# Mixing loop of a hybrid attention and RWKV-7 block: the order of TensorE's work inside one iteration's solve, and the place of the sixth projection

## The chip, the cores and the metric

The kernel runs on one core of one Trainium2 chip. The metric is device time in microseconds (us); runs of one kernel are compared by their median. The engines are TensorE (PE in the profile, with its weight loads as PEld), VectorE (DVE), ScalarE (ACT), GpSimd (POOL) and SyncE (SP), which issues the DMAs. Each engine works through its own instructions in their written order and waits on semaphores.

## The reference, cut to what matters

One layer over a sequence of 1024 tokens of width 1024, all float32:

```python
x += 0.5 * swiglu(rmsnorm(x), w_gate1, w_up1, w_down1)
z = rmsnorm(x) @ w_in                     # q, ak, av, r, k, v, u, ug, gate_a, gate_b
o_a = window_gqa_sinks(q, ak, av, sinks)  # 16 heads, window of two 64-token chunks, ALiBi
o_b = rwkv7_time_mix(r, k, v, ...)        # per head a 64x64 state:
      # sa = state @ a_t
      # state = state * w_t + sa b_t^T + v_t k_t^T ;  y_t = state @ r_t
x += (sigmoid(gate_a) * o_a + sigmoid(gate_b) * o_b) @ w_out
x += cross_attention(rmsnorm(x), rmsnorm(mem))
x += 0.5 * swiglu(rmsnorm(x), w_gate2, w_up2, w_down2)
out = rmsnorm(x)
```

The change touches only the second step, where attention and time mixing are computed together. The time mixing is done in chunks of 64 tokens. Inside a chunk the recurrence is a triangular system, which is solved by doubling the solved blocks (levels 2, 4, 8, 16, 32); from chunk to chunk a 64x64 state is carried in a chain.

## The kernel before, in words

`mixer()` runs 16 iterations (`ITER`), one for each pair of heads (8) and half of the sequence (2 halves of 512 tokens, 8 chunks each), and two more that drain the pipeline. Iteration i does three things at a time: it projects the inputs of pair i+1, it solves the triangular systems of pair i, and it carries the chain and writes the outputs of pairs i-1 and i-2. Every engine has `prepare(i)` and then `solve(i)`.

**Projections.** An iteration has six units (`PROJ`: k, r, v, q, ga, gb). A unit is 24 matmuls of 128x512 on two-part rounded operands (L1171), accumulated in bank P0 or P1 by turns. For each unit SP loads a weight panel, ACT rounds it (`round_panel`, L1442), POOL subtracts to get the low part (`subtract_panel`, L1076), PE multiplies, and ACT stores the result (`store`, L1451, L1455, L1459). In the kernel before, units 0 to 4 are in PE's `prepare`. Unit 5 is done in `solve`, in five pieces of 4 or 5 matmuls, one in each level; ACT stores it, and rounds the panel after next, after its `solve`, and POOL subtracts that panel after its `solve`. Pair 8 (the first of the second half) needs the second half of the normed input, which SP loads into the same buffer as the first one (`load_second_half`, L1048) once the last unit of the first half is projected (`proj_ready` of 48); unit 48 waits for it (`s_half`).

**Solve, head.** Eight slots: (0) the products N and its transpose (64 small matmul instructions each way, banks F0 and F3), (1, 2) b scores in two halves (L1279), (3) b tokens, (4, 5) k scores in two halves (L1279), (6) v tokens, (7) k tokens. ACT copies N (L1533, L1535) and the tokens (L1539, L1542, L1545); DVE masks N (L1756), the b scores (L1721) and the start of the solution (L1724), and the k scores (L1729); POOL masks and completes the start X0 (L1128, L1131) and masks N for each level (L1137).

**Solve, levels.** Five levels of four quarters: Z of chunks 0 to 3, Z of chunks 4 to 7 (PE; ACT copies each, L1557), growth of chunks 0 to 3, growth of chunks 4 to 7 (PE; DVE adds into XT, L1743, and into X, L1749). Z and the growth into XT write from one half of the array to the other (`to_other`, L1291), the growth into X does not (`heads`, L1158), and the two alternate.

**Chain.** The pair before is carried over its 8 chunks in 3 steps each, 24 in all. Step 0 multiplies the old state (ACT copies the product p1, L1550), step 1 solves for sa (ACT copies, L1553), step 2 sums the new state (DVE updates it, L1768). Each step needs the copy or the update of the step before. Step s-4 follows slot s: four steps stand in the head after slots 4 to 7, and in a level the first two stand between the matmuls of the two Z quarters, the third after the first growth and ahead of the piece of the projection, the fourth after the second growth.

**Attention.** The scores of pair i are the first thing in PE's `prepare(i)` (banks F2, F3); DVE scales them (L1614). After them come the two small LoRA products (L1197, L1198).

In `prepare(i)` POOL takes the token differences (L1098) for DVE's mixes (L1601), and two transposes on PE (L1241) wait for a spread that DVE copies (L1677).

Of the kernel before, what the change touches and what calls it, by code (L numbers as in the profile page):

```python
# [35 lines left out]
ALU = mybir.AluOpType  # L36
# [54 lines left out]
def build(nc, d, out, x_spill, m_spill, h_spill, a_spill):  # L91
    table, where = constants()
    ctx = ExitStack()
    with ctx:
# [832 lines left out]
        def mixer():  # L927
# [71 lines left out]
            SCORES, FIRST_CHAIN = 8, 4  # L999
            SLOTS = SCORES + 4 * len(LEVELS)  # L1000
            assert SLOTS == FIRST_CHAIN + 3 * NC
            TERMS = 3 * KT

            def quarter(s):

                return divmod(s - SCORES, 4)
# [13 lines left out]
            with nc.Block() as block:  # L1020
# [49 lines left out]
                def _(pool):  # L1070
# [12 lines left out]
                    def prepare(i):  # L1083
# [39 lines left out]
                        for j in range(3, NP - 1):  # L1123
                            next_panel(i, j)
# [20 lines left out]
                    for i in range(ITER + 2):  # L1145
                        prepare(i)
                        if i < ITER:
                            solve(i)
                        next_panel(i, NP - 1)

                @block.tensor
                def _(pe):
# [7 lines left out]

                    def project(unit, first=0, end=TERMS):

                        if first == 0:
                            pe.wait_ge(S("panel_low"), unit + 1)
                            if unit >= 2:
                                pe.wait_ge(S("proj_stored"), unit - 1)
                        for term in range(first, end):
                            kt, (wp, hp) = term // 3, THREE[term % 3]
                            if unit == NP * PAIRS and term % 3 == 0:
                                pe.wait_ge(s_half[kt], 32)  # L1170
                            last = mm(bank[:, unit % 2, :], pw[wp][:, unit % 2, kt], hA[hp][:, kt],  # L1171
                                      start=term == 0, stop=term == TERMS - 1)
                        if end == TERMS:
                            last.then_inc(S("proj_ready"), 1)

                    def prepare(i):
# [23 lines left out]
                        if more:  # L1200
                            project(first)
# [14 lines left out]
                        if more:  # L1216
                            project(first + 1)
# [37 lines left out]
                        if more:  # L1255
                            project(first + 4)

                    def solve(i):
# [35 lines left out]
                        def score_slot(s):  # L1294
                            every = range(NC)
                            if s == 0:
                                seen("rows_ready", 4, 4)
                                seen("oa_ready")
                                for n in every:
                                    heads(one(F0)[:, n, :], cur[:, n, 0, :], b_ch[:, n, :])  # L1300
                                    last = to_other(one(F3)[:, n, :], cur[:, n, 0, :], b_ch[:, n, :])
                                last.then_inc(S("n_ready"), 1)
                            elif s == 1:
                                scores(F1, b_ch, 0).then_inc(S("b_scores_ready"), 1)
                            elif s == 2:
                                seen("bonus_used")
                                scores(F2, b_ch, 1).then_inc(S("b_scores_ready"), 1)
                            elif s == 3:
                                seen("ends_ready", 2, 2)
                                if i + 1 < ITER:  # L1310
                                    pe.wait_ge(S("proj_stored"), NP * (i + 1) + 4)
                                by_heads(P1, lambda n: b_ch[:, n, :], lambda n: cur[:, n, 2, :],
                                         every).then_inc(S("b_tok_ready"), 1)
                            elif s == 4:
                                seen("x_copied")
                                scores(F3, k_ch, 0).then_inc(S("k_scores_ready"), 1)
                            elif s == 5:
                                if i + 1 < ITER:
                                    pe.wait_ge(S("proj_stored"), NP * (i + 1) + 5)
                                scores(P0, k_ch, 1).then_inc(S("k_scores_ready"), 1)  # L1320
                            elif s == 6:
                                seen("n_stored")
                                seen("n_copied")
                                by_heads(F0, lambda n: vm[:, n * CH:(n + 1) * CH], lambda n: c("stack_ident"),
                                         every).then_inc(S("v_tok_ready"), 1)
                            else:
                                seen("base_stored", 2, 1)
                                by_heads(F1, lambda n: k_ch[:, n, :], lambda n: cur[:, n, 2, :],
                                         every).then_inc(S("k_tok_ready"), 1)

                        def level_slot(n, k, beside=None):
                            q = k % 2
                            chunks = range(4 * q, 4 * q + 4)
                            if k < 2:
                                if n == 0:
                                    seen("xt0_ready", 2, q + 1)
                                    if q == 0:
                                        seen("base_stored", 2, 2)
                                    else:
                                        seen("before_stored", 2, 1)  # L1340
                                else:
                                    seen("n_masked", 4, n)
                                    seen("xt_added", 10, 2 * n - 1 + q)
                                for m, at in enumerate(chunks):
                                    last = to_other(one(ZB[q])[:, m, :], n_st[n % 2][:, at, :], xt_new[:, at, :])
                                    if m == 3:
                                        last.then_inc(S("z_ready"), 1)
                                    if beside and m > 0:
                                        chain_step(*beside, m - 1)
                            else:  # L1350
                                seen("z_stored", 10, 2 * n + 1 + q)
                                if n == 0:
                                    seen("x0_ready")
                                    seen("v_tok_stored")
                                    seen("k_tok_stored")
                                else:
                                    seen("x_added", 8, 2 * n)
                                if q == 1:
                                    seen("xt_added", 10, 2 * n + 1)
                                    if n < 4:  # L1360
                                        seen("x_added", 8, 2 * n + 1)
                                for m, at in enumerate(chunks):
                                    grown = to_other(one(TB)[:, m, :], x_st[:, at, :], z_st[:, at, :])
                                    if m == 3:
                                        grown.then_inc(S("xt_grown"), 1)
                                    if n < 4:
                                        last = heads(one(XB)[:, m, :], z_st[:, at, :], x_st[:, at, :])
                                if n < 4:
                                    last.then_inc(S("x_grown"), 1)
# [36 lines left out]
                        for s in range(SLOTS):  # L1406
# [845 lines left out]
```

## Time and profile before

| | |
|---|---|
| median of 3 runs | 3304.08 us (3301.25 to 3305.58) |
| the profiled execution's own time | 3303.52 us |
| its span in the profile | 3301.7 us |
| PE busy | 2963.9 us, 90% |
| PEld busy | 2434.4 us, 74% |
| DVE busy | 1598.2 us, 48% |
| POOL busy | 1300.2 us, 39% |
| ACT busy | 1055.4 us, 32% |

The first view of the profile gives each engine's busy time over the span. An engine's own waits are in the view of waits, and the order of its instructions, with their starts, in the timeline. The mixing loop takes the stretch from about 863 to 2050 us. Its iterations can be told apart by the two LoRA products (L1197), which begin at 1461.6, 1531.9, 1602.1 us and so on.

### The profile page before, as it was taken

Reading aid. Unit: us, or ns where it says so; the run is one execution under the profiler, and the core shown is the slowest. Engines: PE = TensorE matmul, PEld = TensorE weight load, DVE = VectorE, ACT = ScalarE, POOL = GpSimd, SP = SyncE. Lnnn points to the kernel's source line nnn. Section 1 sums busy time; section 2 is a strip of 40 time slices with the busy share of each in tenths; the row PEclk is TensorE's granted clock in tenths of the full one; section 3 lists DMA queues with packets and bytes.
Section 4 is the critical chain, followed back from the end, with each engine's and each line's share of the span. In section 5 each row is a group of like instructions: output and inputs, shape, how many; then the busy total and the mean of one; then the engine's idle time right before and its main releaser. Section 6 shows DMA issues by size and latency. Waiting matters only on the chain. (4 is left out here: it accounts for less than half of the span.)

```text
span 3301.7 us, 61575 instructions
## 1 busy us (share of the span) xinstructions
PE 2963.9 (90%) x26974; PEld 2434.4 (74%) x26974; DVE 1598.2 (48%) x1747; ACT 1055.4 (32%) x1718; POOL 1300.2 (39%) x667
## 2 busy tenths in 40 slices
PE   3899999996899999999999986797976799999995
PEld 2688888884678877787877765786755588887885
DVE  6654444444166556656655662113222744453445
ACT  2433333222234334433434432212121333333221
POOL 1344444442364545455544541222131344444441
PEclk7999999997999999999999986898988899999997
DMA  3222224433221111322111100611002222234441
GB/s 139 80 96 80 80 103 166 144 121 134 59 62 58 52 45 45 96 63 63 52 45 45 53 21 9 229 52 32 19 26 89 64 80 77 78 108 159 144 144 67
DMA packets 247432, 270.71 MB, mean 82 GB/s; under 512 B 13184, under 2 KB 204800, under 8 KB 245120
## 3 DMA queue, kind: packets, MB, share of 16 engines
q1 hardware_dynamic: 247168, 266.81, 24.6%
q8 instruction: 212, 3.47, 0.4%
q14 instruction: 52, 0.43, 0.0%
HBM read 218.54 MB, written 48.23 MB: 81 GB/s over the span
## 5 line engine op out<-in xcount | busy, mean ns | idle before, releaser
L459 POOL TENSOR_TENSOR w_low<-ffn_work,w_high 128x1024 fp32r<-128x1024 f32 x182 | 445.0, 2446 | 668.6 <-ACT w_high L532 393.9
L499 PE MATMUL bank<-h_high,w_high 128*128 128x512 f32 x1232 | 484.6, 393 | 57.6 <-DVE h_low L643 34.6
L499 PE MATMUL bank<-h_low,w_high 128*128 128x512 f32 x1232 | 483.3, 392 | 0.0
L499 PE MATMUL bank<-h_high,w_low 128*128 128x512 f32 x1232 | 482.9, 392 | 0.0
L1076 POOL TENSOR_TENSOR mix_panel_low<-arena,mix_panel_high 128x1024 fp32r<-128x1024 f32 x96 | 233.0, 2427 | 343.6 <-ACT mix_panel_high L1442 343.6
L1171 PE MATMUL bank<-mix_h_high,mix_panel_high 128*128 128x512 f32 x768 | 317.6, 414 | 20.0 <-POOL mix_panel_low L1076 14.9
L690 DVE TENSOR_TENSOR h_low<-ffn_work,h_high 128x512 fp32r<-128x512 f32 x88 | 205.7, 2337 | 250.7 <-ACT h_high L547 250.7
L499 PEld LDWEIGHTS bank<-h_high,w_high 128*128 128x128 f32 x1232 | 233.9, 190 | 110.9 <-issue 60.1
L1171 PE MATMUL bank<-mix_h_low,mix_panel_high 128*128 128x512 f32 x768 | 304.4, 396 | 0.0
L1171 PE MATMUL bank<-mix_h_high,mix_panel_low 128*128 128x512 f32 x768 | 303.3, 395 | 0.0
L516 PE MATMUL bank<-h_high,w_high 128*128 128x512 f32 x704 | 275.2, 391 | 4.6 <-DVE h_low L690 4.6
L516 PE MATMUL bank<-h_low,w_high 128*128 128x512 f32 x704 | 275.3, 391 | 0.0
L516 PE MATMUL bank<-h_high,w_low 128*128 128x512 f32 x704 | 275.1, 391 | 0.0
L499 PEld LDWEIGHTS bank<-h_high,w_low 128*128 128x128 f32 x1232 | 233.6, 190 | 49.0
L499 PEld LDWEIGHTS bank<-h_low,w_high 128*128 128x128 f32 x1232 | 233.7, 190 | 48.3
L674 DVE TENSOR_TENSOR ffn_work<-bank,ffn_work 128x512 f32<-128x512 f32 x132 | 90.2, 688 | 346.2 <-ACT ffn_work L574 244.5
L459 POOL TENSOR_TENSOR w_low<-arena,w_high 128x1024 fp32r<-128x1024 f32 x60 | 145.1, 2420 | 195.8 <-ACT w_high L532 195.8
L1291 PE MATMUL bank<-arena 64*64 64x64 f32 x5120 | 214.5, 226 | 2.4 <-DVE arena L1749 0.9
L1291 PEld LDWEIGHTS bank<-arena 64*64 64x64 f32 x5120 | 179.2, 134 | 30.8 <-issue 29.0
L1171 PEld LDWEIGHTS bank<-mix_h_high,mix_panel_high 128*128 128x128 f32 x768 | 145.0, 189 | 68.7 <-issue 27.4
L540 ACT ACTIVATE w_high<-ffn_work 128x1024 fp32r<-128x1024 f32 x88 | 93.2, 1059 | 310.4 <-PE bank L516 303.7
L685 DVE TENSOR_TENSOR ffn_work<-ffn_work 128x512 f32<-128x512 f32 x66 | 153.7, 2328 | 69.4 <-ACT ffn_work L584 68.8
(263 smaller groups left out, 5822.8 us busy)
## 6 DMA issues: line engine op xcount, KB each, us to landing
arena<-w_in SPq DMA_DIRECT2D x96, 512.0 KB, 3.8
ffn_work<-w_down SPq DMA_DIRECT2D x88, 512.0 KB, 3.6
a_spill<-ffn_work SPq DMA_DIRECT2D x88, 256.0 KB, 2.3
ffn_work<-a_spill SPq DMA_DIRECT2D x88, 256.0 KB, 2.7
ffn_work<-w_gate SPq DMA_DIRECT2D x12, 1024.0 KB, 5.7
ffn_work<-w_up SPq DMA_DIRECT2D x12, 1024.0 KB, 8.2
arena<-x_spill SPq DMA_DIRECT2D x3, 4096.0 KB, 14.2
arena<-w_gate SPq DMA_DIRECT2D x10, 1024.0 KB, 5.6
```

The lines of the kernel that those rows point to most:

```text
L459: nc.gpsimd.tensor_tensor(slot(w[1], q), src, slot(w[0], q).bitcast(F32), ALU.subtract).then_inc(s_low, 1)
L499: last = mm(bank[:, bk, :], w[wp][:, q % RING, kt, e], h[hp][:, k, kt], start=fresh and kt + wp + hp == 0, stop=kt == KT // 2 - 1 and wp = ...
L516: last = mm(bank[:, BANK_OF[o], :], w[wp][:, (LAST + p) % RING].rearrange("p a b c -> p (a b) c")[:, o], h[ap][:, B11, p % 4], start=p % N ...
L540: A(slot(w[0], LAST + p), panel[p % 4].rearrange("p (a b) -> p a b", b=P), ACT.Copy).then_inc(s_high, 1)
L674: V.tensor_tensor(post[first + e], bank[:, bk[e], :], post[first + e], ALU.add).then_inc(s_added, 1)
L685: ins = V.tensor_tensor(post[at], post[at], post[at + 1], ALU.mult)
L690: V.tensor_tensor(h[1][:, B11, p % 4], a_raw[p % 2], h[0][:, B11, p % 4].bitcast(F32), ALU.subtract).then_inc(s_alow, 1)
L1076: G.tensor_tensor(pw[1][:, unit % 2], raw[unit % 2], pw[0][:, unit % 2].bitcast(F32), ALU.subtract).then_inc(S("panel_low"), 1)
L1171: last = mm(bank[:, unit % 2, :], pw[wp][:, unit % 2, kt], hA[hp][:, kt], start=term == 0, stop=term == TERMS - 1)
L1291: last = mm(hs(out, 1 - e), hs(lhs, e), hs(rhs, e), start=True, stop=True)
```

## The change

The sixth projection (unit 5) moves from the levels of the solve to the end of `prepare`, behind the fifth, as one block; ACT's store and rounding and POOL's subtraction for it move with it. The two halves of the k scores, the v tokens, the k tokens and the attention scores of the next iteration move into the levels, one to each, where the pieces of the projection were (`filler`). The chain's four steps of the head stand one ahead of each of the four remaining parts of the head, and the fourth step of a level stands ahead of the second growth. Banks of some scores change. The core of the diff:

```diff
                     def prepare(i):
...
                         if live:
-                            pe.wait_ge(S("proj_stored"), NP * i + 4)
-                            for n in range(NC):
-                                at = (window + n) * CH
-                                last = heads(two(F2)[:, n, :], q_t[:, n * CH:(n + 1) * CH], kd[:, g, at:at + P])
-                            last.then_inc(S("att_scores_ready"), 1)
+                            if i == 0:
+                                attention_scores(0)
...
                         if more:
                             project(first + 4)
+                            project(first + 5)
...
+                        def filler(n):
+                            if n == 0:
+                                seen("base_stored", 2, 2)
+                                scores(P0, k_ch, 0).then_inc(S("k_scores_ready"), 1)
+                            elif n == 1:
+                                seen("b_tok_stored")
+                                scores(P1, k_ch, 1).then_inc(S("k_scores_ready"), 1)
+                            elif n == 2:
+                                seen("before_stored", 2, 1)
+                                by_heads(P0, lambda n: vm[:, n * CH:(n + 1) * CH], lambda n: c("stack_ident"),
+                                         every).then_inc(S("v_tok_ready"), 1)
+                            elif n == 3:
+                                seen("before_stored", 2, 2)
+                                by_heads(P1, lambda n: k_ch[:, n, :], lambda n: cur[:, n, 2, :],
+                                         every).then_inc(S("k_tok_ready"), 1)
+                            elif i + 1 < ITER:
+                                seen("z_stored", 10, 10)
+                                attention_scores(i + 1)
...
-                            if live and i + 1 < ITER and s >= SCORES and quarter(s)[1] == 2:
-                                n = quarter(s)[0]
-                                if n == 0:
-                                    seen("b_tok_stored")
-                                project(NP * (i + 2) - 1, n * TERMS // 5, (n + 1) * TERMS // 5)
...
+                        if live:
+                            hop(0)
+                            n_products()
+                            hop(1)
+                            b_scores(0)
+                            hop(2)
+                            b_scores(1)
+                            hop(3)
+                            b_tokens()
+                            for n in range(len(LEVELS)):
+                                make_z(n, 0)
+                                make_z(n, 1)
+                                grow(n, 0)
+                                hop(FIRST_HOPS + 4 * n + 2)
+                                filler(n)
+                                hop(FIRST_HOPS + 4 * n + 3)
+                                grow(n, 1)
```

`make_z` keeps two chain steps between the matmuls of the two Z quarters (`hop` 4 and 5 of level 0, and so on). On ACT, POOL and DVE:

```diff
@@ ACT
                         next_unit(4)
+                        next_unit(5)
...
                         if live:
+                            hop(0)
                             seen("n_ready")
                             A(flat(x_st), bank[:, F3, :], ACT.Copy).then_inc(S("x_copied"), 1)
+                            hop(1)
...
-                        if i + 1 < ITER:
-                            store(NP * (i + 2) - 1)
-                            round_panel(NP * (i + 2) + 1)
@@ POOL
-                        for j in range(3, NP - 1):
+                        for j in range(3, NP):
                             next_panel(i, j)
...
-                        next_panel(i, NP - 1)
@@ DVE
+                            store_base(0)
+                            hop(2)
+                            store_base(1)
+                            for n in range(len(LEVELS)):
+                                hop(FIRST_HOPS + 4 * n)
+                                hop(FIRST_HOPS + 4 * n + 1)
+                                level_slot(n, 0)
+                                hop(FIRST_HOPS + 4 * n + 2)
+                                hop(FIRST_HOPS + 4 * n + 3)
+                                if n < 2:
+                                    store_before(n)
+                                level_slot(n, 1)
```

ACT copies the v tokens after the chain steps of level 2 and the k tokens after those of level 3.

## Rows read from the trace of the kernel before

**Rows 1.** Page, busy time of each engine over the span: us, share, instructions.

```profile
PE 2963.9 (90%) x26974; PEld 2434.4 (74%) x26974; DVE 1598.2 (48%) x1747; ACT 1055.4 (32%) x1718; POOL 1300.2 (39%) x667
```

**Rows 2.** Windows, two iterations: length, busy us (instructions), PEclk the granted clock.

```profile
1461.60:1531.90 70.30, 68.50 (x1182) 56.30 (x1180) 43.70 (x65) 28.34 (x59) 35.63 (x23) 1.00 0.18 53
1383.60:1461.60 78.00, 71.52 (x1182) 56.94 (x1180) 41.49 (x66) 28.35 (x59) 34.47 (x23) 0.98 0.35 106
```

**Rows 3.** Waits of PE, 1461.6 to 1954 us (seven iterations): total, times, longest.

```profile
PE bank L1158 <- DVE mix_work L1768: 3.3, 7, 0.5
PE bank L1241 <- DVE mix_work L1677: 3.2, 7, 0.5
```

**Rows 4.** Timeline of PE around one projection piece: start, us, instruction, [idle before].

```profile
1513.56 0.28 PE L1158 MATMUL bank<-mix_work,arena 64*64 64x64 f32 x4
1513.78 0.50 PE L1171 MATMUL bank<-mix_h_low,mix_panel_high 128*128 128x512 f32 x1
1514.12 0.39 PE L1171 MATMUL bank<-mix_h_high,mix_panel_low 128*128 128x512 f32 x1
1514.35 0.40 PE L1171 MATMUL bank<-mix_h_high,mix_panel_high 128*128 128x512 f32 x1
...
1515.14 0.27 PE L1291 MATMUL bank<-arena 64*64 64x64 f32 x2
```

**Rows 5.** Timeline of PE, head of the solve and the first growth.

```profile
1498.32 0.27 PE L1158 MATMUL bank<-mix_work 64*64 64x64 f32 x2
...
1499.30 1.92 PE L1279 MATMUL bank<-mix_work 64*64 64x128 f32 x32
1501.05 1.10 PE L1158 MATMUL bank<-mix_work 64*64 64x64 f32 x32
1501.98 1.04 PE L1279 MATMUL bank<-mix_work 64*64 64x128 f32 x16
...
1507.16 0.27 PE L1158 MATMUL bank<-mix_work,arena 64*64 64x64 f32 x2 [0.17 <-ACT mix_work L1550]
...
1508.12 0.27 PE L1158 MATMUL bank<-arena 64*64 64x64 f32 x2
```

**Rows 6.** Timeline of PE where one level ends and the next begins.

```profile
1511.13 0.28 PE L1291 MATMUL bank<-arena 64*64 64x64 f32 x4
1511.63 0.27 PE L1158 MATMUL bank<-mix_work 64*64 64x64 f32 x2 [0.22 <-ACT mix_work L1553]
...
1515.85 0.28 PE L1291 MATMUL bank<-arena 64*64 64x64 f32 x3
1516.60 0.28 PE L1158 MATMUL bank<-mix_work,arena 64*64 64x64 f32 x2 [0.47 <-DVE mix_work L1768]
```

**Rows 7.** Timeline of DVE and POOL where the next iteration's mix begins.

```profile
1530.81 2.35 POOL L1076 TENSOR_TENSOR mix_panel_low<-arena,mix_panel_high 128x1024 fp32r<-128x1024 f32 x1 [11.60 <-ACT mix_panel_high L1442]
1534.45 1.51 DVE L1601 SCALAR_TENSOR_TENSOR mix_work<-mix_work,arena 128x512 f32<-128x512 f32 x1 [1.25 <-POOL mix_work L1098]
```

**Rows 8.** Timeline of ACT after the fifth projection, and one sa copy.

```profile
1498.43 0.60 ACT L1459 ACTIVATE mix_work<-bank 128x512 f32<-128x512 f32 x1
...
1499.87 0.59 ACT L1533 ACTIVATE arena<-bank 128x512 f32<-128x512 f32 x1
...
1507.54 0.22 ACT L1553 ACTIVATE mix_work<-bank 128x64 f32<-128x64 f32 x1 [0.43 <-PE bank L1158]
```

**Rows 9.** Timeline of DVE in the head of the solve.

```profile
1501.12 1.57 DVE L1724 TENSOR_TENSOR arena<-arena 128x256 f32<-128x256 f32 x1
1502.61 0.68 DVE L1721 TENSOR_TENSOR arena<-bank,arena 128x512 f32<-128x512 f32 x1
...
1505.46 0.28 DVE L1768 SCALAR_TENSOR_TENSOR mix_work<-mix_work,bank 128x64 f32<-128x64 f32 x1 [0.34 <-PE bank L1158]
```

**Rows 10.** Timeline of POOL in the head of the solve.

```profile
1500.05 2.36 POOL L1076 TENSOR_TENSOR mix_panel_low<-arena,mix_panel_high 128x1024 fp32r<-128x1024 f32 x1 [6.35 <-ACT mix_panel_high L1442]
...
1503.72 1.34 POOL L1131 TENSOR_TENSOR arena<-arena 128x512 f32<-128x512 f32 x1
```

**Rows 11.** Timeline of SP and PE where the second half comes in.

```profile
1380.88 0.34 SPq L1048 DMA_DIRECT2D mix_h_high<-h_spill  x1
...
1388.57 0.50 PE L1171 MATMUL bank<-mix_h_high,mix_panel_high 128*128 128x512 f32 x1 [2.99 <-DMA mix_h_low<-h_spill]
```

**Rows 12.** Timeline of PE in the last iteration, whose levels hold no projection.

```profile
1995.94 0.28 PE L1158 MATMUL bank<-mix_work,arena 64*64 64x64 f32 x4
1996.71 0.27 PE L1291 MATMUL bank<-arena 64*64 64x64 f32 x2 [0.48 <-DVE arena L1749]
```

More of the change, by code:

```diff
@@ L1159, in heads, with project, attention_scores @@
                         return last
[L1161 to L1169, printed above, removed]
-                                pe.wait_ge(s_half[kt], 32)
[L1171 to L1174, printed above, removed]
+                    def project(unit):
+                        if unit >= UNITS:
+                            return
+                        pe.wait_ge(S("panel_low"), unit + 1)
+                        if unit >= 2:
+                            pe.wait_ge(S("proj_stored"), unit - 1)
+                        for kt in range(KT):
+                            if unit == NP * PAIRS:
+                                pe.wait_ge(s_half[kt], 32)
+                            for wp, hp in THREE:
+                                last = mm(bank[:, unit % 2, :], pw[wp][:, unit % 2, kt], hA[hp][:, kt],
+                                          start=kt + wp + hp == 0, stop=kt == KT - 1 and wp == 1)
+                        last.then_inc(S("proj_ready"), 1)
+                    def attention_scores(i):
+                        pe.wait_ge(S("proj_stored"), NP * i + 4)
+                        for n in range(NC):
+                            at = (i // PAIRS * NC + n) * CH
+                            last = heads(two(F2)[:, n, :], q_t[:, n * CH:(n + 1) * CH],
+                                         kd[:, i % PAIRS // 4, at:at + P])
+                        last.then_inc(S("att_scores_ready"), 1)
                     def prepare(i):
@@ new lines, in solve, with n_products, b_scores @@
+                        every = range(NC)
+                        def n_products():
+                            seen("rows_ready", 4, 4)
+                            seen("oa_ready")
+                            for n in every:
+                                heads(one(F0)[:, n, :], cur[:, n, 0, :], b_ch[:, n, :])
+                                last = to_other(one(F3)[:, n, :], cur[:, n, 0, :], b_ch[:, n, :])
+                            last.then_inc(S("n_ready"), 1)
+                        def b_scores(q):
+                            if q == 1 and i + 1 < ITER:
+                                pe.wait_ge(S("proj_stored"), NP * (i + 2) - 1)
+                            scores((F1, P0)[q], b_ch, q).then_inc(S("b_scores_ready"), 1)
@@ new lines, in make_z @@
+                        def make_z(n, q):
+                            chunks = range(4 * q, 4 * q + 4)
+                            if n == 0:
+                                seen("xt0_ready", 2, q + 1)
+                                seen("n_stored")
+                                if q == 0:
+                                    seen("bonus_used")
+                                else:
+                                    seen("x_copied")
+                            else:
+                                seen("n_masked", 4, n)
+                                seen("xt_added", 10, 2 * n - 1 + q)
+                            for m, at in enumerate(chunks):
+                                last = to_other(one(ZB[q])[:, m, :], n_st[n % 2][:, at, :], xt_new[:, at, :])
+                                if m == 3:
+                                    last.then_inc(S("z_ready"), 1)
+                                if back and 0 <= m - q < 3:
+                                    chain_step(*divmod(FIRST_HOPS + 4 * n + q, 3), m - q)
@@ new lines, in grow @@
+                            if q == 1:
+                                seen("xt_added", 10, 2 * n + 1)
+                                if n < 4:
+                                    seen("x_added", 8, 2 * n + 1)
+                            for m, at in enumerate(chunks):
+                                grown = to_other(one(TB)[:, m, :], x_st[:, at, :], z_st[:, at, :])
+                                if m == 3:
+                                    grown.then_inc(S("xt_grown"), 1)
+                                if n < 4:
+                                    last = heads(one(XB)[:, m, :], z_st[:, at, :], x_st[:, at, :])
@@ L1371, in outputs @@
+                            if n < 4:
+                                last.then_inc(S("x_grown"), 1)
                         def outputs(n, part=None):
```

193 lines of the change are left out of this document (67 added, 126 removed).

## The prediction

> **What bounds the kernel now.** I read the page first: PE is busy 90% of the span, every other engine under half [rows 1]. Then the windows of single iterations of the mixing loop: one takes 70.3 us, PE is busy in 68.5 of them at full granted clock, and the next engine, DVE, in 43.7 [rows 2]. So PE's own order of work sets the loop's time, and a change that only moves work on the others is worth nothing unless PE waits for them. Third, PE's waits: few and short, some 0.5 us each in every iteration for the chain's state update and for the spread of the variance [rows 3]. The reader should not stop there: a small matmul counts as busy for 0.22 to 0.28 us while the next one can start 0.03 us later, so this view shows a wait only from where the last matmul has drained. The true loss is in PE's timeline, between the starts of neighbours. I therefore price everything from starts.
>
> **Part 1, the sixth projection becomes one block.** Inside a block one matmul starts 0.23 us after the other (1514.12 to 1514.35). A piece of five is entered and left at a price: from the last group of small matmuls (1513.56, four in about 0.12) to the next small one at 1515.14 there are 1.46 us, and five matmuls at 0.23 are 1.14 [rows 4]. That is 0.32 to 0.33 a piece, five pieces an iteration: 1.65 us saved, since at the end of prepare the block follows another projection and adds no border. The 24 matmuls themselves cost the same. The panel for it is rounded after unit 3 and subtracted while unit 4 runs, so PE should not wait for it. The parts put into the levels are the same instructions as before; their work cancels.
>
> **Part 2, chain steps apart.** Where a level ends with a chain step and the next one begins with its successor, PE stands: 1511.13 to 1511.63 for four matmuls worth 0.12, so 0.38 lost to ACT's copy of sa; and 1515.85 to 1516.60, 0.66 lost to DVE's state update [rows 6]. The steps' kinds repeat every three levels, so the first stands twice and the second once in an iteration. With the second growth between the two steps (16 pairs of the N products' kind took 0.98 [rows 5], so its 8 take 0.5) all three go: 2 x 0.38 + 0.66 = 1.42 us. The waits between the two steps of the Z quarters stay as they are, since those steps stay where they were but for one matmul.
>
> **Part 3, the prepare.** POOL's subtraction at 1530.81 stands ahead of the differences, and DVE's first mix waits 1.25 for them and is then slow at 1.51 [rows 7]; after the change POOL has nothing before them and takes them during the solve, so DVE's chain runs about 2 us earlier against PE. The wait for the spread goes (3.2 over seven [rows 3]): 0.45 us. What is late next is DVE's scaling of the attention scores, which now waits only for DVE's last add; it starts 0.3 us later against the LoRA products, well inside the 2 us.
>
> **Part 4, the head, where I expect the losses.** Let T be the start of the first small matmul after the last projection (1498.32). Work: N products 0.98, b scores 0.87 a half, b tokens 0.93, so 0.12 for one pair of heads [rows 5]. ACT is now in front of the first chain copy with the store and the rounding of a panel: it stored at T+0.11 and was free at T+1.55 [rows 8]. PE does hop 0 (two pairs, 0.23) and the N products and stands at T+1.21 at hop 1, which needs p1: copy 0.22, resumed at T+1.83. Loss 0.62. Then hop 1 and b scores to T+2.82, hop 2 to 3.05, b scores to 3.93. Hop 3 needs the state from DVE, and DVE has the first L1721 and L1724 before it. L1721 takes 0.68 and starts at about T+3.0; L1724 took 1.57 and ended 0.28 after POOL's subtraction [rows 9, 10]; POOL ends that at T+4.09 again, so L1724 ends at about T+4.4, the update takes 0.28, PE resumes at T+4.72. Loss 0.8. Then five pairs of hop 3 (0.58) and b tokens, T+6.23. The copy of the b tokens (0.6, like L1459) now stands on ACT just ahead of the copies of hop 4 and Z: a loss of about 0.35 in the second Z. The first growth comes at T+7.7, and X0, which POOL completes at T+6.74 [rows 10], is in time. Before, the first growth was at 1508.12, T+9.8 [rows 5], with 3.6 us of scores and tokens that are now elsewhere and 0.47 of waits, one of them at 1507.16. So waits of 1.77 stand for 0.47: a cost of 1.3 us. Its ends: only X0 binds and the two chain waits vanish, 0.5; or both ACT's queue and DVE's double, 3.0.
>
> **Queues behind the new waits.** On DVE the k scores' mask (0.7) stands ahead of the second adds of levels 0 and 1 and may hold the next Z by 0.25 once; the attention scores must see the last Z copied, 0.1; and with fillers of 0.9 in place of 1.46 some round trips begin to show, 0.2: together 0.55, from 0 to 3.3. The upper end is the last iteration, whose levels have no filler: the second growth waits there from 1995.94 to 1996.71 for DVE's adds, 0.66 more than the four matmuls need [rows 12]; five of these are 3.3. A filler of 0.9 covers 0.66, which is why I stay near the low end.
>
> Sum of an ordinary iteration: -1.65 -1.42 -0.45 +1.3 +0.55 = -1.7 us. Fourteen of them (1 to 14): -24.
>
> A page of the Trainium skill ("SBUF — State Buffer", section "Who interferes with whom") says that a DVE instruction with two SBUF inputs is shut out for the whole of a GpSimd instruction that reads SBUF and began first. The end of L1724 0.28 after POOL's end agrees. By that rule the second L1724, behind L1131, would end only at about T+7.0 and hold the second Z by some 0.2 us, 3 us in all; the forecast leaves this out.
>
> **Part 5, once.** The second half is loaded after the last unit of the first half. That unit ended in the last level of iteration 6: the load's first issue is at 1380.88 and PE still stands for it at 1388.57 [rows 11], and the iteration takes 78.0 instead of 70.3 us [rows 2]. Now the unit ends ahead of the solve, and the solve lay from 1498.32 to the LoRA products at 1531.9 in its like; even cut by 5 us that is far more than the 7.7 us from the first issue to that wait's end, and nothing in that solve reads the buffer. The 7.7 us go but for 0.1: -7.6.
>
> **Part 6, the ends.** The last iteration has no projection, before or after; its levels get fillers where they had none: three waits like the one of rows 12 (2.0) and 1.42 as above, and no panel stands before its head: -3.5. The first has no chain, so it saves the 1.65 and loses about 2 waiting for X0: +0.5.
>
> Total -24 -7.6 -3.5 +0.5 = -34.6, say -35. The profiled execution took 3303.5 us, 0.6 under the median of the three runs, so both give the same: **3268 us**. For this case alone 3258 to 3278.
>
> **The rivals.**
> (a) *The waits move instead of going.* Step 2 saves nothing, because what ends last between levels is DVE's add into XT and not the chain. For it: in rows 12 the adds of a growth reach PE 0.77 after its last group of matmuls, and the second Z now comes about that soon behind the growth. Against: DVE's last add is done before the state update in rows 6. Per iteration -1.65 -0.45 +1.3 +0.55 = -0.25; with parts 5 and 6, -15: 3289 us.
> (b) *The head costs little.* DVE gets L1724 through before POOL and ACT's panel is early: cost 0.5 instead of 1.3, and no 0.55: -3.0 an iteration, -42 -10.6: 3251 us.
> (c) *The levels fall to the round trips (slower).* The fillers of 0.9 don't cover the trip over ACT and DVE between the two growths, and every level waits 0.66 as in rows 12, the chain's saving being taken by the same waits: -1.65 -0.45 +1.3 +3.3 = +2.5 an iteration, +35, less 8 for part 5: 3330 us. It decides from 0.3 us of new waits a level. Against it: the wait without any filler is only 0.66.
> (d) *Nothing much*: the losses of the head are 3.0 and those of the levels 0.7: +0.2 an iteration, less the once-only parts, 3296 us.
>
> **How the numbers follow.** Forecast 0.54, (a) 0.16, (b) 0.20, (c) 0.05, (d) 0.05. The range from 3243 to 3295 leaves out (c), half of (d) and the far side of (b). About 0.2% (6.6 us) is what a measurement can tell from no change. The forecast, (a), (b) and part of (d) are faster by more: 0.91. Within: 0.04. Slower, mostly (c): 0.05.
>
> **What would show it.** An iteration of about 68.6 us between LoRA products; iteration 7 the same as the others, no wait for the spilled half; PE's timeline without the jumps of 0.5 and 0.75 at level borders, but with new ones at hop 1 (ended by ACT's p1 copy) and hop 3 (ended by the state update) in the head; L1171 in blocks only; no wait at L1241. Wrong, if PE waits for a panel ahead of the sixth unit, if the granted clock in the loop falls from 1.00, or if the wait before a second growth appears in each level.

## The result, and the profile after

The changed kernel takes 3325.55 us (median of 5 runs, 3319.22 to 3328.55) against 3303.97 before; the ratio is 1.0064 with a 95% interval of 1.0049 to 1.0078. It is slower by 21.6 us where 35 us less were forecast, and outside the range.

The profiled execution took 3325.55 us, its span is 3323.8 us. The page's row of busy times answers to [rows 1]: PE does the same 26974 matmuls and is busy for less.

```profile
PE 2944.8 (89%) x26974; PEld 2442.2 (73%) x26974; DVE 1571.2 (47%) x1747; ACT 1051.2 (32%) x1718; POOL 1296.7 (39%) x667
```

The windows of one ordinary iteration after, whole and in its three parts (prepare, solve up to the first growth, from there to the LoRA products), answer to [rows 2]. Columns: length, busy us of PE, PEld, DVE, ACT and POOL, granted clock, DMA share, GB/s.

```profile
1544.80:1616.50 71.70, 67.39 (x1178) 56.97 (x1178) 41.66 (x66) 27.79 (x60) 35.30 (x22) 1.00 0.18 51
1586.30:1593.70 7.40, 6.19 (x213) 5.68 (x213) 3.17 (x6) 4.02 (x10) 5.64 (x4) 1.00 0.25 71
1593.70:1616.50 22.80, 19.70 (x761) 18.53 (x752) 7.57 (x28) 6.94 (x24) 7.51 (x8) 1.00 0.01 4
1544.80:1586.30 41.50, 41.50 (x220) 32.77 (x220) 30.91 (x32) 16.83 (x26) 22.15 (x11) 1.00 0.25 74
```

The same three parts of an iteration of the kernel before:

```profile
1461.60:1498.30 36.70, 36.26 (x196) 28.15 (x194) 31.69 (x31) 15.08 (x23) 24.52 (x15) 1.00 0.28 83
1498.30:1508.10 9.80, 9.63 (x309) 9.38 (x308) 5.63 (x8) 5.51 (x13) 6.17 (x4) 1.00 0.20 57
1508.10:1531.90 23.80, 22.61 (x690) 18.78 (x682) 6.37 (x26) 7.75 (x24) 4.94 (x4) 1.00 0.02 4
```

| part of an iteration, us | before | forecast | after |
|---|---|---|---|
| prepare (with the block after) | 36.7 | 41.8 | 41.5 |
| head, to the first growth | 9.8 | 7.7 | 7.4 |
| levels, to the LoRA products | 23.8 | 19.4 | 22.8 |
| sum | 70.3 | 68.9 | 71.7 |

The forecast column is the prediction's own terms, split by place: the levels lose the five pieces (24 x 0.23 and 1.65) and the border waits (1.42), and get 3.6 of scores and tokens and 0.55. Its sum is 0.3 over the prediction's 68.6: the T+7.7 of the head doesn't quite follow from the prediction's own terms, 9.8 - 3.6 + 1.3 = 7.5, and the rest is rounding. Two parts came out within 0.3 us. All of the error is in the levels. What stands there is in the view of PE's waits over seven iterations, which answers to [rows 3]: total, times, longest. Most is given to "issue", time in which the profile shows nothing that PE waited for.

```profile
PE bank L1151 <- issue: 10.1, 17, 1.1
PE bank L1293 <- issue: 5.5, 8, 1.0
PE bank L1151 <- DVE mix_work L1783: 3.2, 7, 0.5
PE bank L1151 <- ACT mix_work L1552: 2.6, 6, 0.4
PE bank L1194 <- DVE arena L1769: 2.1, 7, 0.3
```

In the timeline of PE these stops come in the middle of a growth or between two matmuls of one Z, where no semaphore is waited for. These are the four of one iteration:

```profile
1600.65 0.27 PE L1151 MATMUL bank<-arena 64*64 64x64 f32 x1 [0.75 <-issue]
...
1604.18 0.39 PE L1151 MATMUL bank<-arena,mix_work 64*64 64x64 f32 x7 [0.70 <-issue]
...
1608.16 0.27 PE L1293 MATMUL bank<-arena 64*64 64x64 f32 x1 [0.75 <-issue]
...
1611.74 0.27 PE L1293 MATMUL bank<-arena 64*64 64x64 f32 x2 [0.61 <-issue]
```

Counting all of PE's records between them (matmuls, weight loads and its few semaphore instructions) gives 255, 257 and 255, and in the whole trace every such stop falls on the same remainder of 256 (193 to 195). The page has a queue whose packets fit this count: 3.47 MB in 212 packets is 16 KB each, and PE's 54920 records are 214.5 times 256. In the bare stream below it is 61 packets for 15700 records, 61.3 times 256.

```profile
q8 instruction: 212, 3.47, 0.4%
```

In the trace's packets the block that ends a stop begins its transfer 2.2 to 2.9 us before PE goes on. From starts the four stops are 0.97, 0.92, 0.97 and 0.82 long, 3.5 us more than the steps of small matmuls need. Up to the LoRA products of the last iteration there are 61 "issue" stops of more than 0.3 us, from start to start, between small matmuls, 56.7 us in all; the kernel before has one, of 0.42. The counts of stops below are made in the same way.

**Theory 1**: PE's instructions arrive in blocks of 256, one after the other, each taking some 3.6 us. Small matmuls of 64x64 use a block up sooner, and PE stops for the rest. By this theory the long matmuls of the projection pieces had given this time back. **Theory 2**: the stops are round trips over ACT and DVE that the new order of steps exposes.

### The profile page after: what moved, and what is told of

Same layout as the page of the kernel before. It is cut to its first block and busy times, and to the rows that moved or that the text cites. A ratio compares the mean times of both kernels' runs of the same rounds, so it can differ in the third digit from the quotient of the medians.

```text
span 3323.8 us, 61558 instructions
## 1 busy us (share of the span) xinstructions
PE 2944.8 (89%) x26974; PEld 2442.2 (73%) x26974; DVE 1571.2 (47%) x1747; ACT 1051.2 (32%) x1718; POOL 1296.7 (39%) x667
## 3 DMA queue, kind: packets, MB, share of 16 engines
q8 instruction: 212, 3.47, 0.4%
## 5 line engine op out<-in xcount | busy, mean ns | idle before, releaser
L1070 POOL TENSOR_TENSOR mix_panel_low<-arena,mix_panel_high 128x1024 fp32r<-128x1024 f32 x96 | 240.2, 2503 | 234.2 <-ACT mix_panel_high L1458 234.2
L1151 PE MATMUL bank<-mix_work 64*64 64x64 f32 x3584 | 180.5, 224 | 14.2 <-ACT mix_work L1555 7.2
## 6 DMA issues: line engine op xcount, KB each, us to landing
arena<-x_spill SPq DMA_DIRECT2D x3, 4096.0 KB, 14.4
```

The lines of the kernel that those rows point to most:

```text
L1070: G.tensor_tensor(pw[1][:, unit % 2], raw[unit % 2], pw[0][:, unit % 2].bitcast(F32), ALU.subtract).then_inc(S("panel_low"), 1)
L1151: last = mm(hs(out, e), hs(lhs, e), hs(rhs, e), start=start, stop=stop)
```

## The experiments

**The change with its projection pieces back in the levels.**

```diff
                                 filler(n)
+                                if i + 1 < ITER:
+                                    if n == 0:
+                                        seen("b_tok_stored")
+                                    project(NP * (i + 2) - 1, n * 24 // 5, (n + 1) * 24 // 5)
@@ prepare
-                            project(first + 5)
```

> The changed kernel with one part undone: the sixth projection is back in the levels in five pieces, one behind each filler; ACT's store and rounding and POOL's subtraction for it are back behind the solve. Fillers, head and the even spread of the chain steps stay (k scores and tokens all use bank P0). Theory 1 (supply of PE's instructions: in the changed kernel PE stops for 0.8 to 1.0 us after every 256 of its instructions in the levels, with nothing to wait for, because small matmuls alone use them up faster than blocks of 256 arrive; long matmuls between them give the time back): no such stops, an iteration about 68.9 us, 3280 us. Theory 2 (the stops are round trips over ACT and DVE that the new order exposes): the order of the steps is the same, the stops stay in part, 3300 to 3310 us.

Measured: 3346.0 us, ratio 1.0138 (1.0121 to 1.0155). Both forecasts missed: it is slower than either. The stops between small matmuls fell from 61 to 12 (12.1 us in all), which is theory 1's part. But an ordinary iteration took 72.9 us on average (all but 0, 6 and 7), where 68.9 were forecast. Two things that theory 1's sum had left out were seen. First, prepare is bound by another chain: with the attention scores no longer in front of it and POOL's subtraction back ahead of the differences, PE waits for the spread of the variance again, 7.5 us in seven iterations. Second, where a head and one half level hold no long matmul, a block is still used up too soon: 1.1 us at 1530.91, ahead of the first filler. They don't make up the whole miss: prepare takes 1.6 us more than in the kernel before where 0.45 less was forecast, the stops are 0.8 an iteration, and the rest stays open. The waits of the head (0.43, 0.48, 0.28) are the changed kernel's.

```profile
1512.84 0.66 PE L1241 MATMUL bank<-arena,mix_work 128*128 128x128 f32 x4 [1.07 <-DVE mix_work L1705]
1522.84 0.33 PE L1152 MATMUL bank<-mix_work,arena 64*64 64x64 f32 x4 [0.43 <-ACT mix_work L1551]
1525.64 0.33 PE L1152 MATMUL bank<-mix_work,arena 64*64 64x64 f32 x4 [0.48 <-DVE mix_work L1785]
1528.18 0.27 PE L1152 MATMUL bank<-mix_work 64*64 64x64 f32 x2 [0.28 <-ACT mix_work L1554]
1530.91 0.33 PE L1279 MATMUL bank<-mix_work 64*64 64x128 f32 x2 [1.10 <-issue]
```

So this run does not part the theories by its time; the next ones do.

**The kernel before with the block alone.**

```diff
                             project(first + 4)
+                            project(first + 5)
...
-                                project(NP * (i + 2) - 1, n * TERMS // 5, (n + 1) * TERMS // 5)
```

> The kernel before with only one part of the change: the sixth projection stands in prepare as one block, with ACT's and POOL's work for it; scores, tokens and chain steps stay where they were, so the levels hold nothing but Z, growths and chain. Theory 1 (supply): stops every 256 PE instructions in the levels although the order of the steps is the old one; a level of some 280 instructions takes at least 3.9 us where the work is 3.3; an iteration about 72 us, 3322 us. Theory 2 (round trips): only the waits of the last iteration of before, three of 0.7, less the 1.65 of borders: about 70.7 us an iteration and the once-only gain of 7.6, so 3302 us, and the waits are ended by DVE or ACT.

Measured: 3323.81 us, ratio 1.0071 (1.0055 to 1.0088), iterations mostly of 71 to 73 us. That is theory 1's 3322, but the time was hit in part by luck, for both kinds of loss are there. Up to the last LoRA products the trace has 31 stops of the 256 kind (26.5 us in all from start to start, 1.8 an iteration) and 46 steps of about 0.7 us that DVE's adds end (32.7 us, 2.2 an iteration), which are theory 2's three waits of 0.7 an iteration. Theory 2 alone misses by 22 us, since it has no stops; theory 1's sum left out the waits. The time is about that of the changed kernel, but not its make-up: there the fillers have taken the place of the waits for DVE, and the stops are twice as many. So this run shows the stops in the old order of steps, and not that the new order costs nothing. The timeline of PE in one iteration has both kinds:

```profile
1526.96 0.27 PE L1157 MATMUL bank<-arena 64*64 64x64 f32 x3 [0.56 <-issue]
1527.77 0.27 PE L1291 MATMUL bank<-arena 64*64 64x64 f32 x2 [0.36 <-DVE arena L1742]
...
1536.07 0.21 PE L1291 MATMUL bank<-arena 64*64 64x64 f32 x1 [1.10 <-issue]
```

**The changed kernel with work added.**

```diff
                         def filler(n):
+                            if n < 4 or i + 1 < ITER:
+                                mm(bank[:, (P0, P1, P0, P1, F2)[n], :], c("ident"), uT[:, 0:HALF], start=True,
+                                   stop=True)
```

(with the waits of the filler set ahead of it)

> The changed kernel with work added: each level has one more matmul of 128x512 in float32 (0.86 us and two borders, some 1.15 us in all, only 4 instructions) ahead of its filler, into the filler's bank; its result is overwritten. Nothing else is changed. Theory 1 (supply): the added work falls into the stops, which shrink or vanish, so an iteration grows by about 2 us instead of 5.75: 3357 us. Theory 2 (round trips or any other cost): the work adds up, less what hides a wait between the growths: 3395 to 3412 us.

Measured: 3366.06 us, ratio 1.0201 (1.0184 to 1.0219). Against the changed kernel that is 40.5 us (45 when each is set against the kernel before as it ran beside it) for work that adds up to some 86; an iteration takes 74 to 75 us instead of 72. The stops between small matmuls fell from 61 to 5. About half of the added work cost nothing, as theory 1 has it, though its 3357 was 9 us too low; theory 2's 3395 is 29 off.

**The supply by itself.**

```python
for k in range(1280):
    last = small(k)            # float32, 64x64, the four quarters in turn
    if k % 64 == 63:           # second stream; k % 32 == 31 in the third
        last = long(k // 64)   # float32, 128x512
```

> The disputed cost by itself: a kernel that computes nothing of the reference; PE runs three streams without any wait, each of 1280 float32 matmuls of 64x64 (2560 matmul records, 5120 instructions with the weight loads), all four quarters of the array in turn: the first alone, the second with one 128x512 float32 matmul after every 64 small ones, the third with one after every 32. Theory 1 (supply at some 3.6 us for 256 instructions): about 72, 73 and 75 us, with stops 256 instructions apart in the first. Theory 2 (no limit of supply): 37, 54 and 72 us.

Measured in one run, by the windows of the three streams, in which the first column is the length: 71.2, 74.6 and 84.9 us.

```profile
23.60:94.80 71.20, 41.84 (x2562) 39.23 (x2562) 0.00 (x0) 1.00 0.04 11
101.80:176.40 74.60, 65.59 (x2600) 47.68 (x2599) 0.00 (x0) 1.00 0.02 4
184.30:269.20 84.90, 84.90 (x2640) 52.61 (x2639) 0.00 (x0) 1.00 0.02 4
```

The first two are near theory 1's 72 and 73 and far from theory 2's 37 and 54. The third is over the 75 and the 72: PE never stands there, the stream is its own work, and what it has beyond the 41.8 us of the small matmuls comes to 1.08 us for each long matmul with its borders, not 0.86. The timeline of the first stream shows the blocks bare: 128 matmuls and 128 weight loads in 2.09 us, then nothing until the next 256.

```profile
34.99 2.09 PE L28 MATMUL bank<-rows 64*64 64x64 f32 x128 [1.36 <-issue]
35.00 1.96 PEld L28 LDWEIGHTS bank<-rows 64*64 64x64 f32 x128 [1.50 <-issue]
38.72 2.09 PE L28 MATMUL bank<-rows 64*64 64x64 f32 x128 [1.64 <-issue]
```

From the stop that ended at 28.09 to the one at 93.83 there are 18 blocks: 3.65 us each, the single ones 3.45 to 4.0. This settles the cause of the stops for theory 1; there is no other engine at work in that kernel, and its stops too fall on one remainder of 256 (193). A block's transfer takes 1.0 us and begins 2.3 to 2.7 us before PE goes on, as in the changed kernel.

**One part of the change alone: the fourth chain step ahead of the second growth**, in the kernel before.

```diff
+                                if step and quarter(s)[1] == 3:
+                                    chain_step(*step)
+                                    step = None
                                 level_slot(*quarter(s), beside=beside)
```

> The kernel before with one part of the change alone: the chain's fourth step of each level stands ahead of the second growth (on DVE its state update too, ahead of that growth's adds). The projection pieces stay in the levels. Theory 1 (chain waits at level borders are real, and the supply of PE's instructions is enough while long matmuls stand in the levels): the three waits (1.42 us) go; the levels then take 22 us for about 5.7 blocks of 256 instructions, 3.85 a block against the 3.65 of the measured supply, so at most a short stop: an iteration 69.1 us, 3287 us. Rival (DVE's add into XT ends last at the borders, or the supply takes it back): 70.3 us, 3300 us.

Measured: 3283.92 us, ratio 0.9942 (0.9929 to 0.9956), an iteration of 68.6 to 69.7 us. The border waits of [rows 6] are gone, and the pieces keep PE supplied but for 7 stops (5.9 us). An ordinary iteration takes 69.1 against 70.2 us: 1.3 less in the levels, 0.1 more in prepare, where the wait for the spread grew. Part 2 of the prediction was right, and it pays by itself; so does part 3, in the next run.

**The two side effects alone**: POOL's differences ahead of its last subtraction, and the block in iteration 6 only.

```diff
                                 G.tensor_tensor(mixed[j][:], zraw[:, j, 0:HALF], ...)
+                            if i > 0:
+                                next_panel(i - 1, NP - 1)
@@ PE
                             project(first + 4)
+                            if i == PAIRS - 2:
+                                project(first + 5)
```

> The kernel before with two side effects of the change made on purpose and alone: in iteration 6 only, the sixth projection is a block in prepare, so that the second half of the input loads during that solve; and POOL takes the token differences ahead of its last panel subtraction in every iteration. Theory 1: iteration 7 falls from 78.0 to 70.3, iteration 6 rises by about 1.8 (stops every 256 instructions in its levels), and the wait for the spread (0.45) goes from each: 3301 - 6 - 6 = 3289 us. Rival (the spread is late for another reason): 3295 us.

Measured: 3291.91 us, ratio 0.9965 (0.9951 to 0.9978), as forecast, but by another sum. Ordinary iterations took 69.6 (0.7 less, where 0.45 was expected). Iteration 7 fell to 69.7, but iteration 6 rose from 70.3 to 77.3, not by 1.8. The two together gained 1.3 us, no more than two ordinary iterations do by the differences: the early load by itself gained nothing. In iteration 6 the blocks of instructions came late beside the 4 MB:

```profile
1364.25 0.21 PE L1160 MATMUL bank<-arena 64*64 64x64 f32 x1 [1.66 <-issue]
...
1371.17 0.27 PE L1160 MATMUL bank<-mix_work 64*64 64x64 f32 x2 [3.20 <-issue]
```

The stops are not the whole of it. Right behind the one of 3.20 us the granted clock fell from 1.00 to 0.50 (from the 2.4 to the 1.2 GHz level), from 1371.6 to 1378.4 us. The window of iteration 6 has it at 0.96 on average, with PE busy for 70.07 us, where it is 68.35 in iteration 5:

```profile
1310.90:1388.20 77.30, 70.07 (x1182) 59.15 (x1180) 42.50 (x66) 28.41 (x59) 36.44 (x23) 0.96 0.33 102
```

**All of these in one.**

> The kernel before with the fourth step moved and both side effects (the two kernels above in one). Theory 1: the gains add, 3273 us. Rival (once the waits are gone, the supply of PE's instructions limits the levels): 3280 us or more, with stops 256 instructions apart in ordinary iterations.

Measured: 3273.44 us, ratio 0.9914 (0.99 to 0.9927). The gains add; ordinary iterations take 67.7 to 68.7, iteration 6 takes 77.0, with two stops of over 2 us and the granted clock at 0.93 on average.

**The load by tiles.** The same, but iteration 6 keeps its pieces, and each part of the second half is loaded once the piece that used its place is done.

```diff
                         for kt in range(KT):
+                            if kt < 6:
+                                sp.wait_ge(S("tiles_used"), (1, 2, 2, 3, 4, 4)[kt])
+                            elif kt == 6:
+                                sp.wait_ge(S("proj_ready"), NP * PAIRS)
```

> The kernel before with the fourth step of the chain moved and the differences ahead of the panel subtraction, as in the kernel of both; in iteration 6 the sixth projection stays in its five pieces, and each part of the second half is loaded as soon as the piece that used its place is done. Theory 1 (blocks of PE's instructions queue behind the data of a large load and then cost whole microseconds; with the load spread over the levels and long matmuls in them there is slack): iterations 6 and 7 about 69 and 70 us in place of 77.0 and 68.5, 3267 us. Rival (the load costs its 7 us wherever it stands): 3273 us or more.

Measured: 3267.78 us, ratio 0.9902 (0.9884 to 0.992): the fastest of all, 34 us under the kernel before. The windows of iterations 6 and 7 and of an ordinary one show the load's cost gone, and the granted clock at 1.00 throughout. Two things changed at once here (the load in parts, the pieces back in iteration 6), and which of them did it was not tried apart. Iterations 6 and 7 take 8.5 us less than in the kernel of both, but iterations 2 to 5, whose order of work is the same in both, take 3.9 more, with four stops against one, so less than that shows in the time:

```profile
1304.30:1372.80 68.50, 67.71 (x1182) 56.21 (x1180) 43.27 (x66) 28.20 (x59) 35.19 (x23) 1.00 0.32 94
1372.80:1441.30 68.50, 68.16 (x1182) 56.38 (x1180) 42.98 (x66) 28.19 (x59) 35.21 (x23) 1.00 0.26 76
1577.60:1645.70 68.10, 67.82 (x1182) 56.50 (x1180) 43.01 (x65) 28.20 (x59) 35.64 (x23) 1.00 0.19 55
```

**The supply beside a load.**

> Computes nothing of the reference. PE runs the stream of 1280 small float32 matmuls twice without any wait inside: once with no other traffic, once while SP loads 4 MB again and again. Theory 1: about 71 us the first time (3.65 us for 256 instructions) and far more the second time, 5 us or more for 256 instructions, 100 us or more. Rival (the supply does not mind data traffic, and the stops of 2 to 3.4 us in iteration 6 have another cause): 71 us both times.

Measured in one run, the window of the quiet stream and that of the one beside the load (PEclk before the last two columns):

```profile
23.20:93.40 70.20, 41.88 (x2562) 39.22 (x2561) 0.00 (x0) 1.00 0.02 4
113.30:220.70 107.40, 63.01 (x2560) 60.22 (x2560) 0.00 (x0) 0.69 0.80 302
```

107.4 us against 70.2; from 120.38 to 218.74 there are 18 blocks, 5.46 us each. The granted clock goes between 1.00 and 0.50 there, 0.69 on average; it first fell at 104.2, while PE stood 12.87 us for the load's first part. The lower clock is not the cause: a block's matmuls took 2.1 to 3.7 us, at most about the 3.65 of a quiet block, and PE still stood 2 to 5 us ahead of most blocks. The transfer of a block took as long as without the load (median 1.02 against 1.03 us) and began as long before PE went on (2.3 to 2.6 us). What grew is the time between one transfer's start and the next, 5.44 us on average: a block begins its transfer later.

```profile
141.60 3.59 PE L30 MATMUL bank<-rows 64*64 64x64 f32 x128 [2.63 <-issue]
147.52 2.83 PE L30 MATMUL bank<-rows 64*64 64x64 f32 x128 [2.33 <-issue]
```

## Why the prediction was wrong

- **Parts 1 and 3, prepare: right.** 41.5 against 41.8 us. The wait for the spread is gone, DVE's mix takes 0.74 us and waits for nothing. No run shows the border price of a piece alone, but the levels' sum closes with it: 23.8 - 5.5 - 1.65 - 1.4 + 3.6 and the 3.9 of stops and LoRA wait named below make 22.7, and 22.8 were measured. The saving of 1.65 us was bought by taking away what the pieces did besides.
- **Part 4, the head: right in mechanism and size.** The first growth came at T+7.4 (forecast 7.7), with the three waits where the sum had them, at hop 1 (ACT), hop 3 (DVE's update) and in the second Z (ACT):

```profile
1588.07 0.33 PE L1151 MATMUL bank<-mix_work,arena 64*64 64x64 f32 x4 [0.43 <-ACT mix_work L1552]
...
1590.88 0.33 PE L1151 MATMUL bank<-mix_work,arena 64*64 64x64 f32 x4 [0.49 <-DVE mix_work L1783]
...
1593.42 0.27 PE L1151 MATMUL bank<-mix_work 64*64 64x64 f32 x2 [0.28 <-ACT mix_work L1555]
```

- The late end of the second L1724, at T+7.0, which the prediction names and leaves out of its sum, did not come: that instruction (L1750 here) ended at T+5.6. It began before POOL's completion of X0 (L1125) instead of behind it.
- **Part 2, the chain's borders: right**, shown alone by the fourth-step kernel (-1.3 us in the levels, forecast -1.42).
- **The step that failed is "Queues behind the new waits"** with its 0.55 us an iteration. It bounded what the shorter fillers cost by round trips over DVE, and no term of the sum asked whether PE's instructions would be there. Measured in its place: four stops, 3.5 us an iteration; and 0.4 for the LoRA products, which write the bank of the last growth and so wait for DVE's last add now that the attention scores no longer stand between them. Less the 0.55, that is 3.35 of the 3.4 us by which the levels missed. It was in no rival: (c) had the right place and sign, and its time is 4 us off the measured one, but for the wrong cause, and so by luck: its waits would have been ended by DVE.
- **The wording "The parts put into the levels are the same instructions as before; their work cancels" was half true.** Time on PE cancels. Instructions do not: the pieces gave 24 matmuls in 7.1 us, the fillers that took their place give 96 in 3.6. With its weight loads and semaphore instructions the levels went from 1373 to 1514 of PE's instructions; at 3.65 us for 256 that is 19.6 us of supply in the 23.8 before, and 21.6 where the forecast had 19.4.
- **Part 5 was mis-sized.** Iteration 7 lost its 6.5 us, but iteration 6 took 74.7, 2.7 more than its neighbours, with stops of 2.1 and 1.9 us beside the load. In the kernel with the block in iteration 6 alone the exchange was 7.0 for 8.3, and 1.3 of the gain is due to POOL's differences.
- **Part 6.** The first iteration grew by 4.3 us, not 0.5: it has three stops (3.4 us from start to start), and waits for DVE's start of the solution (0.59 and 0.55) and for ACT's copy of Z (0.49); none is put down to X0. The last took 0.8 less to its last growth, not 3.5; it has four stops. In both kernels a part of it, 24 us before and 17 after, is at a granted clock of 0.50, so its terms can't be told apart.
- The sum: the twelve ordinary iterations took 70.2 us before and 71.6 after, 1.4 more each in place of 1.7 less. With iterations 6 (+4.4) and 7 (-6.5) the fourteen took 14.4 more. The first and the last add 3.5, and the 4.2 that are left of the 22.1 between the two spans lie ahead of the loop (1.0) and behind it (3.2); their cause is open.

## What to carry to other kernels

Count instructions, not only time: a stretch in which TensorE uses 256 of its instructions (matmuls, weight loads and semaphore instructions together) in under the 3.65 us measured here runs at the pace at which they arrive, and moving a few long matmuls out of it gives their time back as stops. "Issue" stops that lie a fixed count of instructions apart are the sign, and adding a long matmul that costs little is the test. A large load beside a dense stretch made the blocks come late (two stops of 1.66 and 3.20 us) and the granted clock fell behind the stops; in parts, among long matmuls, the same load cost nothing that could be seen. And a time that comes out as forecast does not show the cause: count each kind of wait in the trace too, as the kernel with the block alone shows.

## What the runs showed of the hardware

- PE's instructions come in blocks of 256: in the nine full kernels and the two bare ones every stop of over 0.3 us between small matmuls that nothing else ends falls on the same remainder. A page of the Trainium skill ("Runtime: NRT & Kernel Launch", section "Instruction fetch mechanics") says the same of the blocks, and the stops 256 instructions apart agree. It also says that the cost of crossing into the next block is mostly hidden. By that the levels would have taken the 19.4 us of the forecast; they took 22.8, and the bare stream of small matmuls took 71.2 us for 20 blocks of 2.1 us of work. Here the measurement decides.
- With no other traffic a block came every 3.45 to 4.0 us, mean 3.65; beside a load of about 300 GB/s every 5.46. The block's own transfer takes no longer there, it only begins later. What holds it back was not tried.
- One float32 matmul of 128x512 among small ones, with its borders, took 1.08 us (the third bare stream).
- The granted clock fell from 1.00 to 0.50 behind PE's long stops: for 6.8 us behind the one of 3.20 us in iteration 6, where PE was then busy for 1.7 us more than in an ordinary iteration.
